# Attention in groups of two pairs of heads, with the scaling of the probabilities on GpSimd

## What is computed

```python
def nsa_attention(...):            # first network, once in each of two layers, 8 heads of width 64
    o_c = softmax(q @ kc.T * scale) @ vc        # keys compressed to 31 blocks
    o_s = softmax(masked(q @ k_s.T * scale)) @ v_s
    o_w = softmax(masked(q @ k_w.T * scale)) @ v_w
    return g0 * o_c + g1 * o_s + g2 * o_w       # gates by token, head and branch

def conformer_conv(...):           # the layer norm that is worked in beside nsa_attention
    u = causal_dwconv(ga * sigmoid(gb), dw_w, dw_b)
    mu = mean(u); var = mean(square(u - mu))
    return silu((u - mu) * rsqrt(var + EPS) * ln_g + ln_b) @ w_pw2

def mixer_ab(...):                 # second network, layer 0
    oa = softmax(qa @ ka.T * scale) @ va                     # A: 8 heads, all 512 keys
    ob = softmax(concat(masked(qb @ kb.T * scale), sink)) @ vb   # B: window of 128, with a sink
def mixer_cd(...):                 # second network, layer 1
    oc = softmax((q_nope @ k_nope.T + q_rope @ k_rope.T) * scale) @ v_c   # C: 64 + 32 wide
    od = softmax(q @ k.T * scale + bias) @ v                 # D: neighbourhood, bias and mask
def memory_cross_attention(...):   # second network, both layers: 4 heads, 256 keys (X2)
```

## Time and profile before

| | |
|---|---|
| median of 3 runs | 2278.95 us (2278.51 to 2280.58) |
| span of the profiled execution | 2275.0 us |
| median less that span | 3.95 us |
| PE busy | 2199.9 us, 97% of the span |
| DVE, ACT, POOL busy | 1246.9, 1078.0, 853.7 us (55, 47, 38%) |
| POOL's L2212 | 618 instructions, 824.7 us |
| chain of waits by engine | PE 85%, DVE 10%, issue 3%, ACT 2%, POOL 1% |
| PE's L1090 (turns) | 864 instructions, 34.2 us idle ahead of them |

### The profile page before, as it was taken

One profiled execution on the slowest core, in us unless ns is written; L12 is line 12 of the kernel. 1 busy time (PEld: TensorE's weight loads), 2 busy tenths in 40 slices (PEclk: granted clock), 3 DMA queues, 4 the chain that ended last, 5 costly groups with the idle time before them and its releaser, 6 DMA issues.

```text
span 2275.0 us, 33281 instructions
## 1 busy us (share of the span) xinstructions
PE 2199.9 (97%) x12130; PEld 1763.7 (78%) x12130; DVE 1246.9 (55%) x2614; ACT 1078.0 (47%) x2160; POOL 853.7 (38%) x665
## 2 busy tenths in 40 slices
PE   8999899999999999989999999999999999999997
PEld 6778667888866788668888888888767888888886
DVE  6997782499778446885552112234666655211222
ACT  6542484465247652685453223343566545322332
POOL 4333304443330343104255545554110425554553
PEclk9999899999999999999999999999999999999998
DMA  5334002332410233203233333343110323333331
GB/s 171 85 91 141 25 2 79 104 91 79 144 38 11 75 89 109 68 2 110 67 94 96 95 109 98 92 124 95 48 60 20 111 66 97 94 95 100 98 96 66
DMA packets 107186, 189.74 MB, mean 83 GB/s; under 512 B 12049, under 2 KB 22801, under 8 KB 106897
## 3 DMA queue, kind: packets, MB, share of 16 engines
q1 hardware_dynamic: 101136, 178.67, 27.3%
q10 hardware_dynamic: 5888, 8.95, 1.2%
HBM read 182.85 MB, written 2.10 MB: 81 GB/s over the span
## 4 chain that ended last, share of the span: by engine, by line
PE 85%; DVE 10%; issue 3%; ACT 2%; POOL 1%; DMA 0%; SPq 0%; DVEq 0%; ACTq 0%
PE bank L861 23%; PE bank L863 23%; PE bank L862 23%; PE bank L1090 3%; PE bank L1103 3%; PE bank L1076 2%; DVE temp L1933 1%; DVE bank L2053 1%; PE bank L868 1%; DVE temp L1965 1%; PE bank L1067 1%; PE bank L1070 1%; PE bank L931 1%; DVE temp L1967 1%; POOL w_lo L2212 1%
## 5 line engine op out<-in xcount | busy, mean ns | idle before, releaser
L2212 POOL TENSOR_TENSOR w_lo<-w_raw,w_hi 128x512 fp32r<-128x512 f32 (+3 forms) x618 | 824.7, 1341 | 1337.1 <-ACT w_hi L1226 1336.7
L861 PE MATMUL bank<-op_hi,w_hi 128*128 128x512 f32 x1840 | 734.4, 399 | 9.1 <-POOL w_lo L2212 4.4
L863 PE MATMUL bank<-op_hi,w_lo 128*128 128x512 f32 x1840 | 719.4, 391 | 0.0
L862 PE MATMUL bank<-op_lo,w_hi 128*128 128x512 f32 x1840 | 719.4, 391 | 0.0
L1226 ACT ACTIVATE w_hi<-w_raw 128x512 fp32r<-128x512 f32 (+2 forms) x634 | 385.4, 617 | 682.5 <-PE bank L863 678.8
L861 PEld LDWEIGHTS bank<-op_hi,w_hi 128*128 128x128 f32 x1840 | 347.1, 189 | 95.7 <-issue 15.3
L862 PEld LDWEIGHTS bank<-op_lo,w_hi 128*128 128x128 f32 x1840 | 347.6, 189 | 73.4 <-issue 4.1
L863 PEld LDWEIGHTS bank<-op_hi,w_lo 128*128 128x128 f32 x1840 | 347.1, 189 | 73.7
L1648 DVE TENSOR_TENSOR temp<-bank,rstd 128x512 f32<-128x512 f32 x151 | 104.4, 691 | 396.0 <-PE bank L863 378.2
L861 PE MATMUL bank<-side_hi,w_hi 128*128 128x512 f32 (+1 forms) x628 | 233.2, 371 | 2.5 <-DVE side_lo L1730 1.4
L863 PE MATMUL bank<-side_hi,w_lo 128*128 128x512 f32 (+1 forms) x628 | 230.9, 368 | 0.0
(11 more groups left out here) (269 smaller groups left out, 2256.3 us busy)
## 6 DMA issues: line engine op xcount, KB each, us to landing
w_raw<-in_weights SPq DMA_DIRECT2D x620, 256.0 KB, 2.7
w_raw<-in_weights SPq DMA_DIRECT2D x32, 192.0 KB, 2.3
temp<-temp SPq DMA_DIRECT2D x40, 64.0 KB, 2.0
x_t<-in_x SPq DMA_DIRECT2D x8, 256.0 KB, 5.4
conv_area<-in_mem ACTq DMA_DIRECT2D x2, 1024.0 KB, 5.5
out_y<-ybuf SPq DMA_DIRECT2D x8, 256.0 KB, 2.1
conv_area<-in_bias ACTq DMA_DIRECT2D x1, 1920.0 KB, 8.0
conv_area<-in_bias ACTq DMA_DIRECT2D x2, 960.0 KB, 4.9
```

What stands on the lines that cost most here:

```text
L861: pe.matmul(dst, w[0], m[0], start=start, stop=False)
L862: pe.matmul(dst, w[0], m[1], start=False, stop=False)
L863: return pe.matmul(dst, w[1], m[0], start=False, stop=stop)
L2212: pool.tensor_tensor(w_lo[:, j, 0:n], w_raw[:, p % RAW_RING, 0:n], w_hi[:, j, 0:n].bitcast(F32), ALU.subtract).then_inc(*mark("weights_spl ...
```

## The change

It regroups the attention in NSA, AB2, D2 and C2; X2 keeps its order.

- **Groups.** A step on PE now takes a group of two pairs (four tiles): scores of group s, then values of group s - 2, then turns of group s - 1. The outputs of A, B, C and D gather four tiles, so that one copy of 256 columns takes them, where two of 128 did. In C the pairs of heads j and j + 1 alternate, and `latent_scores` emits the first part of both pairs and then the second part of all four tiles, which lie in four quarters of PE's rows.
- **Engines.** DVE keeps the reciprocal; POOL does the scaling (new lines L2343 with the gate, L2345 without). DVE copies tiles 1 and 3 of each group out of their turn banks (L2072), ACT tiles 0 and 2 (L1501).
- **Banks.** Score banks are 1, 2, 3, 0 throughout. The turns of a group go to banks 4, 5, the group's own output bank, and 4 again; in NSA, until tile 44 (groups 0 to 10), to 4, 5, 4, 5, and then to 4, 5, 7, 4. The layer norm and the last gate strip move from bank0 to bank7. The copies have four buffers as before, the last of them `rstd`; the probabilities have eight, where they had six.
- **POOL's program.** It was the loop over pieces with the layer norm behind a strip. Now each attention has its own loop there: the scaling of both pairs, the squares and sums of the layer norm cut into steps, and, in the step that holds moment 10, the pieces of the strips that follow (`w_lo`), 2 of them in NSA, 4 in AB2 and C2.
- **The rest.** The warm matmuls in the middle of NSA go, one is added ahead of the first turn in AB2; the drain lists and gate chunks are cut for the new steps; a chunk of C2 is split after the stage and not in it; the last copies on ACT in NSA stand ahead of the table load for silu.

```diff
+PAIRS = {"NSA": 2, "AB2": 2, "D2": 2, "C2": 2, "X2": 1}
-TURN_LAG = 2
-VALUE_LAG = 3
+TURN_LAG = {1: 2, 2: 1}
+VALUE_LAG = {1: 3, 2: 2}
+VECTOR_COPIES = (1, 3)
-SCORES = (1, 2, 3)
-GATE_CHUNKS = (2, 1, 1, 4)
+SCORES = (1, 2, 3, 0)
+GATE_CHUNKS = (2, 2, 4)
-WARM_TURN = {"NSA": {30: 3}, "AB2": {0: 1}, "D2": {0: 2}, "C2": {0: 2}, "X2": {0: 2}}
+WARM_TURN = {"NSA": {}, "AB2": {0: 2}, "D2": {0: 2}, "C2": {0: 2}, "X2": {0: 2}}
...
+                    t["out"], t["out_held"] = (6, at_group - 1) if step[1][0] == "NSA" else (6 + at_group % 2, at_group - 2)
+                        third = t["out"] if step[1][0] != "NSA" else 7 if n >= LN_TILES else 4
+                        t["turn"] = (4, 5, third, 4 if third != 4 else 5)[n % 4]
...
+                def latent_scores(group):
+                    parts = ((0, 0), (0, 1), (1, 0))
+                    for pair in group:
+                        free_banks(pair)
+                        for x, y in parts:
+                            for t in pair:
+                                pe.matmul(score_bank(t), t["q"][x], t["k"][y], start=(x + y == 0), stop=False)
+                    for x, y in parts:
+                        for t in group[0] + group[1]:
+                            ins = pe.matmul(score_bank(t), t["more"][0][x], t["more"][1][y], start=False, stop=(x == 1))
...
-                    pe.wait_ge(*after("probs", a))
+                    pe.wait_ge(*after("probs_scaled" if scaled_by_pool(part, t) else "probs", a))
...
+                for s in range(steps_of(part)):
+                    if part[0] == "C2" and s < len(groups):
+                        latent_scores(groups[s])
+                    else:
+                        for pair in in_group(groups, s):
+                            scores(pair)
...
+                    if 0 <= s - len(groups) < 3:
+                        drain(part, steps[s - len(groups)])
+                    if PAIRS[part[0]] == 2:
+                        for pair in in_group(groups, s - value_lag):
+                            values(pair)
+                    for pair in in_group(groups, s - turn_lag):
+                        for t in pair:
+                            turn(t)
...
+                def scaled(pair):
+                    pool.wait_ge(*after("sums_inverted", pair[1]["a"]))
+                    total, _ = pair_sums(t)
+                    for r, t in enumerate(pair):
+                        e = E[t["a"] % E_RING][:, 0:t["nk"]]
+                        if t["gate"] is not None:
+                            ins = pool.tensor_scalar(e, e, total[:, r:r + 1], t["gate"], ALU.mult, ALU.mult)
+                        else:
+                            ins = pool.tensor_scalar(e, e, total[:, r:r + 1], None, ALU.mult)
+                        ins.then_inc(*mark("probs_scaled", t["a"]))
+                for s in range(steps_of(part)):
+                    if part[0] == "NSA" and s == 7:
+                        norm_squares(l, 0, 2)
+                    for pair in in_group(groups, s - 1):
+                        if scaled_by_pool(part, pair[0]):
+                            scaled(pair)
+                    if NEXT_SPLIT in moments_of(part, s):
+                        split_to(last_of(FOLLOWS[part] + 1))
```

More of the change, by code:

```diff
@@ L1960, in normed @@
                         return
+                    if scaled_by_pool(part, t):
+                        dve.reciprocal(total, total).then_inc(*mark("sums_inverted", a))
+                        return
                     settle(dve.reciprocal(total, total))
@@ L1998, in extra_stage @@
+                    for i in moments_of(part, s):
+                        for stage in between.get(i - LOW_LAG[PAIRS[part[0]]], ()):
+                            if stage[0] in LATE_LOWS:
+                                extra_stage(*stage)
+                        for stage in between.get(i, ()):
+                            if stage[0] not in LATE_LOWS:
+                                extra_stage(*stage)
             def extra_stage(kind, l, c=None):
```

348 lines of the change are left out of this document (217 added, 131 removed).

## The result

The changed kernel takes **2368.11 us** (median, 2365.92 to 2374.29), the kernel before 2279.76 in the same comparison: ratio 1.0396, 95% interval 1.0379 to 1.0413. That is 88 us up, and the forecast was 31 down. The time lies far outside the range.

The account below looks back on a forecast made before the run. PE was taken as the bound in NSA, AB2 and D2, with DVE binding AB2's second half. NSA -12.8, AB2 -5.7, D2 -5.5, C2 -7.2 and X2 0 summed to -31.2, from 2278.95 to 2247.8 us; range 2236 to 2267.

Parts of the forecast that it names:

- the price of the scaling on POOL: POOL's scaling of one 128x512 tile: 0.65 us taken, with 0.61 and 1.38 as ends.
- The loop 4d + 1.56: Least time of a group: four scalings of d each plus turn, copy, reciprocal and engine gaps; 4.16 us at d 0.65.
- The merge in A: First half of AB2: merging two pairs saves PE three fixed parts, 0.56 us; 8 merges, -4.5 us.
- B: Second half of AB2, bound by DVE: about -0.2 us a pair, -3.2 over 16 pairs.
- D2, a small miss: Stage D2: merges -4.5 us, shorter waits for scalings -1.6, start +0.6; sum -5.5.
- Rival 2: POOL's scaling at 1.38 us makes the loop the bound, 7.08 a group; 2289 us, chance 0.04.
- the bank waits: NSA: third turn waits for bank 4, about 0.46 us in groups 0 to 10, 0.15 in seven later; +6.1.
- the end: End of NSA: PE stands about 6.5 us where it stood 3.4, then longer at low clock; +3.9 a layer.
- the middle and what follows: Layer norm in NSA: idle time from some 6.5 to 4.5 us, part of the -3.5 a layer.
- the low clock: NSA's layer norm middle: low-clock cost from some 3.5 to 2 us, part of the -3.5 a layer.
- Rival 3: DVE and POOL take turns at memory, also where DVE reads a bank; 7.15 a group in A, 2290 us, chance 0.04.
- low end: Whole kernel: scaling at 0.61 us, NSA's bank waits hidden (-6) and C2's fill halved; 2236 us.

Follow-up runs that it names:

- two_ops: The changed kernel with a second operation, a multiplication by 1.0, in POOL's scaling outside NSA; 2289.29 us, ratio to before 1.0042.
- one_op_constant: The changed kernel with POOL's scaling outside NSA as one operation by constant 1.0, leaving out the division by row sums; 2359.42 us (one run).
- loop_cut: The changed kernel with DVE's copy of a group's tile 3 moved behind the next group's first reciprocal; 2321.18 us, ratio to before 1.0186.
- two_ops_ln_spread: two_ops with the layer norm factor's spreading one group step later and NSA's four splits in one group step each; 2272.69 us, ratio to before 0.9975.
- two_ops_nsa_before: two_ops with NSA back as in the kernel before: single pairs, scaling on DVE, old banks, warm matmuls; 2261.8 us, ratio to before 0.9920.

## Why the prediction was wrong

**The failed step** is the price of the scaling on POOL. It was taken as 0.65 us, by the cast (0.612), because it reads one tile and writes one. With two operations that is right: 0.694 outside NSA in two_ops, 0.773 with the gate in NSA. With one operation, which is how the change writes it in AB2, D2 and C2, it is 1.567, above even the 1.38 that I had as the end of the range. The near line rate for one input, which the prediction cited beside its choice (d near 0.6), came for the form with two operations and not for the one with one. The trace before held no POOL instruction of this kind on a wide tile in either form. two_ops and one_op_constant show that the form alone decides. The sign that the prediction named for this, turns that wait for the scaling in every group, is what the timeline shows. Between the changed kernel and two_ops it makes 36.2 us in AB2, 23.1 in D2 and 22.8 in C2: 82 of the 120 us between the forecast (2247.8) and the result (2368.1). NSA has 33 more.

**Right, with sizes.** The loop 4d + 1.56 (7.75 worked out, 7.86 measured, and cut in loop_cut). The merge in A: 0.46 (5.90 to 5.44) for 0.56; only the turns of a group came out dearer, 1.94 for 1.86. B: 9.51 us for four pairs (1009.34 to 1018.85 in two_ops), where 10.60 less four times 0.2 gives 9.80. C2: 62.4 for 62.0, with a group at 6.32 (1731.46 to 1737.78) for 6.23. The four second parts do run side by side: three passes over four tiles take 0.91 us from start to the values behind them, as three over two did (0.89).

```profile
1733.04 0.51 PE L1111 MATMUL bank<-side_hi 32*128 32x512 f32 x4
...
1733.61 0.41 PE L1111 MATMUL bank<-side_hi,side_lo 32*128 32x512 f32 x4
1733.95 1.20 PE L1162 MATMUL bank<-temp,vz 128*64 128x128 f32 x17
```

**D2, a small miss.** It came to 53.0 for 49.8: PE's idle time there stayed near 3.8 us, where I had taken 1.6 off, and its work fell by 2.5 where the merges were to give 4.5. DVE scales D's bias there (L1918), before in four single instructions of 1.15 us with a pair's maxima between them, now two in a row, ahead of a group's first reciprocal. The second of two such places in two_ops:

```profile
1664.06 2.34 DVE L1918 SCALAR_TENSOR_TENSOR conv_area<-conv_area 128x960 f32<-128x960 f32 x2
...
1666.69 2.71 POOL L2345 TENSOR_SCALAR temp<-temp,small 128x512 f32<-128x512 f32 x4 [5.23 <-DVE small L2053]
...
1667.53 2.65 PE L1149 MATMUL bank<-consts,temp 128*128 128x128 f32 x16 [0.93 <-POOL temp L2345]
```

PE waits 0.93 us for the first scaling, and the turns, each behind its own, take 2.65 where they take 2.00 unhindered. Eight merges at A's 0.46 are 3.7, less 1.3 for the two blocks of stretched turns 2.4, which is near the 2.5 by which the work fell.

With the fast form AB2, D2 and C2 take 206.2 us where 203 was forecast and before 221.4.

Rival 2 named the right mechanism, the loop with a slow POOL, and the right sign. It had 0.04 and 2289, since its d was 1.38 and its clock full: PE's waits in every group also brought the clock to 0.89 in AB2 and D2 (windows above), where it was 1.00.

**NSA: the second miss, of its own.** Forecast -6.4 a layer, measured +8.0 and +12.4. PE's idle time in layer 0 went from 10.3 to 23.2. By the marks on the timeline:
- the bank waits, ten for ACT's copy of 0.25 each, came to 2.6 us, forecast 6.1;
- the end came to 6.0, forecast 6.5;
- the middle and what follows came to 13, forecast 4.5: the 4.1 of the layer norm, 2.2 behind the four low parts, two stretches of 3.9 and 2.0 around the compressed tiles, whose scaling stands on DVE behind a pair's maxima, and 0.9 ahead of their last values. The step that failed here: I read the moments of the loop as places in time. They are numbers of tiles, and a step of a group takes four, so that small work which lay in two or three steps of pairs falls into one;
- PE's work (its busy time less what windows of 4 us charge to the low clock) fell from 92.6 to 84.7 with 2.84 of warm matmuls in it, so by this estimate the merges gave 5.1 us, not 10.1: 0.28 a merge. A's 0.56 was carried over to blocks that are narrower or of compressed tiles, and turns that wait for late scalings stretch here as in D2; how much is due to each was not worked out;
- the low clock cost more where 1.5 us less was forecast: it was granted at 0.90 and 0.84, before at 0.92.

Not settled: in two_ops_ln_spread NSA takes 112.1 and 115.0 us without the 2.84 of warm matmuls, in two_ops_nsa_before 111.9 and 111.3 with them. How much of this remaining loss of 3 to 6.5 us a layer is the longer idle chain around the compressed tiles, and how much the clock, is open. Moving the compressed tiles' scaling was not tried.

**Contention.** Rival 3's rule, that DVE and POOL take turns where DVE reads a bank, did not come: L2072 and L2026, which read banks, keep 0.69 while POOL scales (L2026 at 980.69 in two_ops, with POOL at work from 980.27 to 982.97). Where DVE reads and writes the common memory, POOL's work can hold it up, as it did L1965 in the earlier trace rows. DVE's scaling of compressed tiles in the changed kernel, first with POOL in the last of its scalings and then its squares (2.09 us), then with POOL idle:

```profile
272.14 0.70 DVE L2046 TENSOR_TENSOR small<-small,gates 128x4 f32<-128x4 f32 x2
272.88 2.08 DVE L2049 TENSOR_TENSOR temp<-temp,small 128x128 f32<-128x128 f32 x2
...
308.98 0.24 DVE L2046 TENSOR_TENSOR small<-small,gates 128x4 f32<-128x4 f32 x2
309.25 0.49 DVE L2049 TENSOR_TENSOR temp<-temp,small 128x128 f32<-128x128 f32 x2
...
272.72 2.09 POOL L2322 TENSOR_TENSOR conv_area<-conv_area 128x512 f32<-128x512 f32 x2
```

2.08 against 0.49 us, and L2046 0.70 against 0.24; POOL's squares keep their 1.04 each. DVE lost about as much in the kernel before, beside POOL's L2212 (single instructions of L1955 and L1958 took 1.28 and 1.32 us for 0.16 and 0.29), so charging nothing for it was near the truth. The 2.08 against 0.49 agrees with the Trainium skill's "GPSIMD Engine Reference", section "Specifications", on the shared interfaces with two inputs in that memory.

One sum of the prediction doesn't hold as written, without bearing on this: its low end. From 2247.8, 6 us and half of C2's 3.3 give 2240, twice 6 (two layers) and that half 2234, and not 2236.

## What to carry to other kernels

An instruction that an engine has not run yet in this form has no price in the trace, however near its neighbours look: write it in a form that the trace does show, or measure it alone, before a loop is built on it. When steps are merged, list every small item by the step it falls into and look for a producer and its reader, or several blocks of one engine, in the same step: it happened three times here, with the layer norm's factor, the four low parts and D's bias. And before work moves to another engine, write down the loop that passes through it and the price at which it binds: that sum held even where the price was wrong.

## What the runs showed of the hardware

- **POOL's TENSOR_SCALAR with one operation is over twice as slow as with two**: 1.567 against 0.694 us for 128x512 fp32 in place, 2.5 against 0.84 ns a column; a constant factor doesn't help (1.492). A second multiplication by 1.0 is the cure (694, 585 and 478 ns for 512, 384 and 256 columns in two_ops, for 1567, 1246 and 927). I had not expected an added operation to save time.
- **The clock of equal work differs between executions.** NSA of layer 0 is the same program in the changed kernel and in one_op_constant, with some 23 us idle in both, and took 118.8 us at a granted clock of 0.90 in the changed kernel's trace and 126.3 at 0.82 in that of one_op_constant:

```profile
242.10:368.40 126.30, 103.75 (x896) 0.82 0.02 6
```

A stage with gaps is thus uncertain by several us, which is why differences of 3 us between variants of NSA stand above only with their intervals.
